# Gate and up projections by a seven-product block scheme, with the weight sums on VectorE

## The reference, cut to what matters

```python
for l in range(DEPTH):                      # DEPTH = 1, D_MODEL = 1024, D_FF = 2816
    h = rms_norm(x, norm_mix[l])
    ...                                     
    x = x + merged @ w_out[l]
    h = rms_norm(x, norm_ffn[l])
    x = x + (jax.nn.silu(h @ w_gate[l]) * (h @ w_up[l])) @ w_down[l]
return rms_norm(x, norm_final)
```

## Time and profile before

| | |
|---|---|
| median of three runs | 1140.46 us |
| the profiled execution, its own time | 1147.27 us |
| span of its slowest core (core 3, the one shown) | 1145.7 us |
| spans of the other cores | 1136.1 to 1139.3 us |
| granted TensorE clock, mean of core 3 | 0.996 of 2.4 GHz |
| PE busy | 1121.7 us (98%) |
| DVE busy | 475.8 us (42%) |
| ACT busy | 305.6 us (27%) |
| POOL busy | 79.1 us (7%) |

### The profile page before, as it was taken

The page is one execution under the profiler, slowest core; times in us unless marked ns, Lnnn a source line. Parts: engine busy times, 40 slices in busy tenths (PEclk is TensorE's granted clock), DMA queues, the critical chain, the costliest instruction groups (busy, mean ns, idle before and its releaser), DMA issues.

```text
span 1145.7 us, 14700 instructions; the slowest of 8 cores (1136.1 to 1145.7 us)
## 1 busy us (share of the span) xinstructions
PE 1121.7 (98%) x5574; PEld 542.3 (47%) x5574; DVE 475.8 (42%) x482; ACT 305.6 (27%) x490; POOL 79.1 (7%) x153
## 2 busy tenths in 40 slices
PE   7999999998999999999999999999999999999998
PEld 3666545453454444444444444444444444444444
DVE  5453554553656556553545622111334211111223
ACT  5434444224212323421212110112432111111111
POOL 1110100100100010001000101111000000000000
PEclk9999999998999999999999999999999999999999
DMA  9999881688498989335415543999967354200133
GB/s 244 172 203 162 132 206 47 114 147 107 83 191 195 258 150 173 61 106 111 76 39 107 95 142 103 219 175 173 173 154 193 102 126 77 37 1 1 37 112 109
DMA packets 78916, 146.34 MB, mean 128 GB/s; under 512 B 46571, under 2 KB 46571, under 8 KB 78592
## 3 DMA queue, kind: packets, MB, share of 16 engines
q0 software_dynamic: 21456, 77.64, 40.1%
q1 hardware_dynamic: 57392, 67.78, 21.7%
HBM read 185.27 MB, written 23.07 MB: 182 GB/s over the span
## 4 chain that ended last, share of the span: by engine, by line
PE 90%; DMA 4%; DVE 3%; ACT 1%; issue 1%; SPq 0%; DVEq 0%; ACTq 0%
PE ps L228 90%; DMA arena<-hb 3%; DMA arena<-x 1%; ACT tmp L419 1%; DVE tmp L390 0%; DVE hb L331 0%; DVE tmp L470 0%; DVE smx L416 0%; PE ps L343 0%; DVE tmp L383 0%; DVE arena L397 0%; ACT tmp L387 0%; ACT hA L352 0%; SPq L177 0%; DVE tmp L483 0%
## 5 line engine op out<-in xcount | busy, mean ns | idle before, releaser
L228 PE MATMUL ps<-hA,ring 128*128 128x512 bf16 (+3 forms) x2496 | 509.0, 364 | 9.1 <-DMA ring<-w_in 5.1
L228 PEld LDWEIGHTS ps<-hA,ring 128*128 128x128 bf16 x2496 | 243.7, 98 | 266.8 <-issue 14.2
L228 PE MATMUL ps<-arena,ring 128*128 128x512 bf16 (+1 forms) x1600 | 330.7, 366 | 0.8 <-ACT tmp L419 0.8
L228 PEld LDWEIGHTS ps<-arena,ring 128*128 128x128 bf16 x1600 | 156.5, 98 | 170.5 <-issue 1.1
L228 PE MATMUL ps<-arena 128*128 128x512 bf16 (+1 forms) x854 | 181.3, 374 | 0.0
L629 DVE TENSOR_TENSOR arena<-ps,tmp 128x1024 bf16<-128x1024 f32 x44 | 53.9, 1225 | 227.9 <-PE ps L228 223.9
L228 PEld LDWEIGHTS ps<-arena 128*128 128x128 bf16 x854 | 83.5, 98 | 96.3
L625 ACT ACTIVATE tmp<-ps 128x1024 f32<-128x1024 f32 x44 | 45.1, 1025 | 253.5 <-PE ps L228 253.5
L470 DVE TENSOR_TENSOR tmp<-tmp 128x1024 f32<-128x1024 f32 (+6 forms) x40 | 49.2, 1230 | 41.1 <-ACT tmp L460 38.6
L228 PE MATMUL ps<-ring,arena 128*128 128x512 bf16 x256 | 57.9, 379 | 0.2 <-issue 0.2
L218 POOL DMA_DIRECT2D ring<-w_in x48 | 25.6, 541 | 442.3 <-PE ps L228 333.4
(11 more groups left out here) (98 smaller groups left out, 585.3 us busy)
## 6 DMA issues: line engine op xcount, KB each, us to landing
ring<-w_in POOLq DMA_DIRECT2D x48, 512.0 KB, 12.9
ring<-w_gate_up POOLq DMA_DIRECT2D x44, 512.0 KB, 12.2
arena<-x SPq DMA_DIRECT2D x32, 512.0 KB, 7.2
tmp<-x_scr SPq DMA_DIRECT2D x24, 512.0 KB, 4.8
x_scr<-arena SPq DMA_DIRECT2D x16, 512.0 KB, 3.3
out<-tmp SPq DMA_DIRECT2D x15, 512.0 KB, 3.1
arena<-w_down POOLq DMA_DIRECT2D x11, 512.0 KB, 24.6
ring<-w_kv POOLq DMA_DIRECT2D x8, 512.0 KB, 18.6
```

Of the source, the lines that this page charges most:

```text
L228: ins = e.matmul(o, l, r, start=s0, stop=s1)
```

## The change

`gu_g` and `gu_u` give way to `gate_up`. Weights and input of a chunk are taken as 2 by 2 blocks (gate and up by channel blocks 0 to 3 and 4 to 7; channel halves by token halves), and the four output blocks come from seven products of four matmuls, 28 instead of 32, over three banks, two of which take two products each. Sums of input blocks are made once for a half (`x_sums`): three go into ring slots that are held from then on, two are written over blocks of `HA`. Sums of weight blocks (`w_sums`) are made for each chunk on DVE while the chunk before it runs, in two parts: `one` and `two`; three blocks go into the space of `kT` or `vT`, two are written over their slot. Each chunk's products are combined by ACT and DVE. The last multiplication of a chunk is put behind the next chunk's second ACT copy (`late`), its silu behind the next chunk's first (`late_act`). The output tiles of half 1 move to chunks 2 to 5, the norms of half 1 all go beside the down tiles, and the last norm of `ffn(0)` goes behind the first sums of `ffn(1)`.

```diff
@@ -165,7 +165,7 @@
     PS = nc.alloc_psum_tensor("ps", [P, 4096], F32)
     plan = Plan()
     st = {"slot": 0, "pb": 0, "stat": 0, "hb": 0, "sm": 0}
-    held = set()
+    held, slots_held = set(), set()
 
     def act(fn, reads, writes):
         plan.op("act", fn, reads=reads, writes=writes)
@@ -205,6 +205,8 @@
             return (self.kind, self.i)
 
     def slot_new():
+        while st["slot"] % RING in slots_held:
+            st["slot"] += 1
         s = Ref("S", st["slot"] % RING)
         st["slot"] += 1
         return s
@@ -620,14 +622,124 @@
...
-    def gu_g(c, s):
-        u = Unit(lambda kc: rg(s, kc * P, (kc + 1) * P), s, (H0.rhs, H0.keys)).run()
-        act(lambda e: e.activation(out=T[c % 2][:, 0:TM], in_=u.ps(), func=AF.Silu), u.keys(), [("T", c % 2)])
-
-    def gu_u(c, s):
-        u = Unit(lambda kc: rg(s, 1024 + kc * P, 1024 + (kc + 1) * P), s, (H0.rhs, H0.keys)).run()
-        dve(lambda e: e.tensor_tensor(out=actT[:, c, :], in0=u.ps(), in1=T[c % 2][:, 0:TM], op=ALU.mult),
-            u.keys() + [("T", c % 2)], kA(c))
+
+    xq = {}
+
...
+
+    def x_slots():
+        for n in ("11+22", "21+22", "11+12"):
+            xq[n] = slot_new()
+            slots_held.add(xq[n].key()[1])
+
+    def x_sums(p):
+        x11, x12, x21, x22 = x_view(0, 0, p), x_view(0, 1, p), x_view(1, 0, p), x_view(1, 1, p)
+        lo, hi = [("HA", p + 1)], [("HA", p + 5)]
+
+        def dst(n):
+            return ring[:, xq[n].key()[1], :].rearrange("p (k t) -> p k t", k=4)[:, :, p * P:(p + 1) * P]
+
...
+        tt(dst("11+22"), x11, x22, ALU.add, lo + hi, [xq["11+22"].key()])
+        tt(dst("11+12"), x11, x12, ALU.add, lo, [xq["11+12"].key()])
+        n2 = dst("21+22")
+        dve(lambda e: e.scalar_tensor_tensor(out=n2, in0=x21, scalar=-1.0, in1=x22, op0=ALU.mult, op1=ALU.subtract),
+            hi, [xq["21+22"].key()])
+        tt(x12, x12, x22, ALU.subtract, lo + hi, lo)
+        tt(x21, x21, x11, ALU.subtract, lo + hi, hi)
+
+    wx = [kT[:, :, :].rearrange("p k t -> p (k t)"), vT[:, :, :].rearrange("p k t -> p (k t)")]
+    wxk = [[("kT",)], [("vT",)]]
+
+    def w_sums(c, s):
+        e_, ek = wx[c % 2], wxk[c % 2]
+        sk = [s.key()]
+        w = rg(s, 0, SW)
+        pairs = w.rearrange("p (a b) -> p a b", a=2)
+        w11, w22 = rg(s, 0, 512), rg(s, 1536, 2048)
+        quads = w.rearrange("p (a b) -> p a b", a=4)
+        mid = rg(s, 512, 1536).rearrange("p (a b) -> p a b", a=2)
+        def one():
+            dve(lambda e: e.tensor_tensor(out=e_[:, 0:1024], in0=pairs[:, 0, :], in1=pairs[:, 1, :], op=ALU.add), sk, ek)
+
+        def two():
+            dve(lambda e: e.tensor_tensor(out=e_[:, 1024:1536], in0=w11, in1=w22, op=ALU.add), sk, [("wA", c % 2)])
+            dve(lambda e: e.tensor_tensor(out=mid, in0=quads[:, 0:4:2, :], in1=quads[:, 1:4:2, :], op=ALU.subtract), sk, sk)
+        return one, two
+
+    late, late_act = [], []
+
+    def gate_up(c, s, Q, sums):
+        e_, ek, wa = wx[c % 2], wxk[c % 2], [("wA", c % 2)]
+        q4, q5, q3, q1, q2 = Q
+        T4, T5, T3, T1, T2 = [T[q] for q in Q]
+        k5, k3, k1 = [("T", q5)], [("T", q3)], [("T", q1)]
+        ks, kt, k2l, k2r = [("T", q4)], [("q4r", q4)], [("T", q2)], [("q2r", q2)]
+        lo, hi = [("HA", t) for t in range(1, 5)], [("HA", t) for t in range(5, 9)]
+        bA = banks(3)
+        bC, bD = bA + 1, bA + 2
+
...
+        def prod(b, w, x, first):
+            mms = [(bank(b), w[0](k), x[0](k), first and k == 0, k == 3) for k in range(4)]
+
+            def fn(e):
+                ins = None
+                for (o, l, r, s0, s1) in mms:
+                    ins = e.matmul(o, l, r, start=s0, stop=s1, skip_group_check=True)
+                return ins
+            plan.op("pe", fn, reads=w[1] + x[1], writes=kB(b, 1))
+
+        def cp(o, b, wr, fn=AF.Copy, sc=1.0, rd=()):
+            act(lambda e: e.activation(out=o, in_=bank(b), func=fn, scale=sc), kB(b, 1) + list(rd), wr)
+
...
+        L, R = slice(0, 512), slice(512, 1024)
+        prod(bC, ws_(512), xh(1, 1), True)
+        cp(T4[:, L], bC, ks)
+        while late_act:
+            late_act.pop(0)()
+        prod(bD, ws_(1536), xs_("11+12"), True)
+        tt(T4[:, R], bank(bD), T4[:, L], ALU.add, kB(bD, 1) + ks, kt)
+        if sums:
+            sums[0]()
+        prod(bA, we(1024, wa), xs_("11+22"), True)
+        tt(T5[:, L], bank(bA), T4[:, R], ALU.subtract, kB(bA, 1) + kt, k5)
+        prod(bD, ws_(1024), xh(0, 0), False)
+        cp(T1[:, L], bD, k1)
+        while late:
+            late.pop(0)()
+        if sums:
+            sums[1]()
+        prod(bC, ws_(0), xs_("21+22"), False)
+        prod(bA, we(512, ek), xh(0, 1), True)
+        two = T5[:, L].unsqueeze(1).broadcast_to((P, 2, 512))
+        o2 = T3[:, 0:1024].rearrange("p (a b) -> p a b", a=2)
+        ac = bank(bA, 2).rearrange("p (a b) -> p a b", a=2)
+        tt(o2, ac, two, ALU.add, kB(bA, 2) + k5, k3)
+
+        def silu():
+            cp(T2[:, R], bC, k2r + k2l, AF.Silu, -1.0, k3)
+            act(lambda e: e.activation(out=T2[:, L], in_=T3[:, L], func=AF.Silu), k3, k2l)
+        late_act.append(silu)
+        prod(bD, we(0, ek), xh(1, 0), False)
+        tt(T1[:, R], bank(bD), T3[:, R], ALU.add, k3 + kB(bD, 1), k1)
+        late.append(lambda: tt(actT[:, c, :], T1[:, 0:TM], T2[:, 0:TM], ALU.mult, k1 + k2l + k2r, kA(c)))
...
@@ -871,8 +983,20 @@
...
+    gu0 = []
+
     def s_hook(j, pos):
         s_tail()
+        if j in (4, 5) and pos == 2:
+            if j == 4:
+                x_slots()
+            x_sums(2 * (j - 4))
+            x_sums(2 * (j - 4) + 1)
+        if j == 6 and pos == 0:
+            gu0.extend(slot_load(w_gu_d[c]) for c in range(2))
+        if j == 7 and pos == 1:
+            for w in w_sums(0, gu0[0]):
+                w()
 
     def merge(hf, H, first):
...
-    sO = [slot_load(w_out_d[q]) for q in range(4)]
+    sO = []
     for i in range(3):
         o_load(1, i)
     TB = [2, 3, 4, 5, 6]
+    roles = [[0, 1, 2, 3, 4, 5, 6], [0, 1, 2, 3, 4, 5, 6]]
...
+    CO = (0, 4, 1, 5, 2, 6, 3, 7)
+
     def ffn(hf):
-        gu = [slot_load(w_gu_d[c]) for c in range(4)]
-        cp, cq = [], []
+        gu = list(gu0)
+        while len(gu) < 4:
+            gu.append(slot_load(w_gu_d[len(gu)]))
+        gu0.clear()
+        if hf == 0:
+            sO.extend(slot_load(w_out_d[q]) for q in range(4))
         for c in range(NF):
-            if c + 4 < NF:
-                gu.append(slot_load(w_gu_d[c + 4]))
             if hf == 0 and c in WD:
                 q = 2 * WD.index(c)
                 dst = atoms(NF + q, 2)
                 plan.op("pool", lambda e, dst=dst, q=q: e.dma_start(out=dst, in_=w_down_d[:, q * D:(q + 2) * D]),
                         writes=kA(NF + q, 2), dma=True)
-            gu_g(c, gu[c])
-            o1(hf, 2 * c)
-            gu_u(c, gu[c])
-            o1(hf, 2 * c + 1)
-            if hf == 0 and NF - 8 <= c < NF - 5:
-                cq.append(x1_load(1, c - NF + 8))
-            if hf == 0 and NF - 6 <= c < NF - 3:
-                q = cq.pop(0)
-                n_ = Norm(T[q][:, 0:D], [("T", q)])
-                cp.append((n_.finish(), c - NF + 6))
+            r = roles[hf]
+            gate_up(c, gu[c], r[:3] + r[3 + 2 * (c % 2):5 + 2 * (c % 2)],
+                    w_sums(c + 1, gu[c + 1]) if c + 1 < NF else None)
+            if c >= 2 and hf == 0 and 2 * c - 4 < NT:
+                while late_act:
+                    late_act.pop(0)()
+                o1(hf, 2 * c - 4)
+                o1(hf, 2 * c - 3)
+            if c + 4 < NF:
+                gu.append(slot_load(w_gu_d[c + 4]))
+        for w in late_act + late:
+            w()
+        late.clear()
+        late_act.clear()
+        cq, cp, cx = [], [], []
+        ydq = [x1_load(hf, 0)]
         if hf == 0:
-            cq.append(x1_load(1, 3))
-            nxt = [3, 4]
-        ydq = [x1_load(hf, 0)]
+            cq = [(x1_load(1, t), t) for t in CO[0:2]]
         for i in range(NT):
             b = banks(2)
+            if hf == 0:
+                for p in cx:
+                    x_sums(p)
+                cx = []
+                for b_, t in cp:
+                    c_trans(b_, t)
+                    if t >= 4:
+                        cx.append(t - 4)
+                cp = []
+                if 1 <= i <= 4:
+                    for q2, t in cq:
+                        cp.append((Norm(T[q2][:, 0:D], [("T", q2)]).finish(), t))
+                    cq = [(x1_load(1, t), t) for t in CO[2 * i:2 * i + 2]]
+                if i == 1:
+                    gu0.extend(slot_load(w_gu_d[c]) for c in range(4))
+                if i == NT - 1:
+                    for w in w_sums(0, gu0[0]):
+                        w()
 
             def grp(kcs, nbs=(0, 1)):
                 return [(bank(b + nb), actT[:, kc, i * P:(i + 1) * P], wdT[:, kc, nb * 512:(nb + 1) * 512],
@@ -994,26 +1145,21 @@
                 continue
```

(56 more changed lines are left out.)

## The result

The changed kernel takes **1121.49 us** (median of four, 1120.12 to 1121.98) against 1140.53 for the kernel before beside it: the ratio is **0.9831, 95% interval 0.9818 to 0.9843**, 19 us less. The forecast was 1121. The profiled execution took 1121.98 us, its span is 1120.4 (core 0).

The account below looks back on a forecast made before the run. PE's matmul count was taken to bound these stages. Terms -22.9 (shorter chunks), +0.6 (start of `ffn(0)`) and +2.6 (moved norm) gave -19.7 us, from the median 1140.46 to 1121; range of 8 in 10: 1112 to 1136.

Parts of the forecast that it names:

- Part 1: Gate and up chunks: 4 of 32 matmuls go in each of 44 chunks, 38.0 us off; PE's chunk 6.04 us.
- Part 2: DVE's load per gate and up chunk: fast bf16 sums, 6.34 us, 6.03 with joins, as long as PE's 6.04.
- Part 3: Latency chain inside a gate and up chunk: period 6.385 us instead of 6.906, 22.9 us gained over 44 chunks.
- The wait at P4: PE's wait before each chunk's fourth product, until DVE's addition has read its bank: 0.31 us in every chunk.
- the 13.6 and the 1.5: Of the 38.0 us, 13.6 lost to waits before the fourth product, 1.5 to waits for the second weight-sum part.
- Part 4 and 7: Output tiles of half 1 in chunks 2 to 5, and input sums in merge and down tiles: both cost 0.
- Part 5: Start of `ffn(0)`: the merge's last DVE operation delays chunk 0's first DVE addition, 0.6 us lost.
- Part 6: Moved norm in `ffn(1)` chunk 0: it delays the weight sums and chunk 1's first product, 2.6 us lost once.
- Part 8: Weight loads with nine slots left: they land in time, room 2.4 us at the least; cost 0, at most 3.
- rival C: Weight loads come late in the gate and up burst: +14 us, 1135; chance 0.06.
- Rivals B and D: Longer DVE joins and releases: 1130 to 1135, chance 0.13; falling clock: 1123, or far over 1140 with chance 0.03.
- Rival D: Clock falls behind PE waits: +2.4 us after the 2.6 wait, 1123; from 0.3 us waits far over 1140, chance 0.03.

Follow-up runs that it names:

- the late P7: Changed kernel with a chunk's seventh product issued behind the next chunk's second and DVE's order changed: stages -14.3 us, ratio to the kernel before 0.9732.
- the two moves: Changed kernel with the seventh product late, DVE reordered and the last norm's ACT part early: stages -14.7 us, ratio to before 0.9711, again 0.9785.

## Why the prediction was right

**Part 1.** Right: 5398 weight loads against 5574, and 6.04 us per chunk is reached as soon as the waits go.

**Part 2.** Right on the point on which the sign hung. `one`, the short sum and the long one last 0.68, 0.416 and 0.692 us; forecast 0.692, 0.425, 0.692. The first half of the perf-mode rule that the prediction cites from the Trainium skill (VectorE: DVE Perf Modes, the perf-mode tier table), which no row of before could show, holds here: 692 ns for 1024 bf16 elements. The joins too: 958.47 - 957.87 = 0.60 for an operation of 0.69.

**Part 3.** Right in kind, 1% off in size. The wait at P4 is 0.25 to 0.31 against 0.31, the period 6.32 against 6.385. What the hand schedule shows with 0.03 at the next P1, and what I read as a small rest, is in truth the second way, of the same length: removing the "13.6 us of the P4 wait" alone gives nothing. That reading of the 13.6 and the 1.5 as two separate losses is the step that was wrong, though the period and the sum do not rest on it.

**Part 4 and 7.** Output tiles and input sums cost nothing; the cover of the sums is larger than what they need.

**Part 5.** Forecast 0.6, measured 0.7: T4R of the first chunk starts 2.78 after the first product (651.50 to 654.28; forecast 2.69), and the chunk takes 7.06 instead of 6.32. The list names 0.86 for P4's wait there and 0.15 for an ordinary one.

**Part 6.** Forecast 2.6; the list names 2.37, and by the spacing of the products it is 2.5. Its cause, the reciprocal behind ACT, is shown. What I missed is the next chunk: ACT loads its table before its first silu, 1.28 us, the product of the chunk before gets late, and with it the sums; PE waits 0.51 in `ffn(0)` and, on the four cores whose clock stayed up, 0.50 in `ffn(1)`. The rows, in `ffn(1)`:

```profile
906.24 1.28 ACT L708 ACT_TABLE_LOAD   x1
...
908.96 1.22 DVE L711 TENSOR_TENSOR arena<-tmp 128x1024 bf16<-128x1024 f32 x1 [0.56 <-ACT tmp L738]
...
911.46 0.81 PE L703 MATMUL ps<-hA,ring 128*128 128x512 bf16 x3 [0.50 <-DVE ring L670]
```

**Part 8 and rival C.** No wait of DVE or PE in these loops names a DMA. POOL did run into its limit of eight, but the weights were there.

**Rivals B and D.** The joins and releases were as the rows said. The clock did not fall in the steady chunks. Behind the one wait of 2.4 us it did, on four of eight cores, and it cost them 0.7 to 1.0 us; on core 0, the one that the page shows, the products step by 0.86 again from 904.45 on. Rival D had allowed for this with up to 2.4. In all the runs that have that wait (2.4 us and more) the clock fell there on four to eight cores, and in the five that do without it on none. The Trainium skill's case of frequent short waits that lower the clock (TensorE: Matmul & The Clock Gate, A second HAM failure mode) did not come up with some forty waits of 0.3 us.

**The number.** That 1121 met 1121.49 so closely is in part luck. The stages gained 1.1 us more than forecast. The shorter period gives some 2.5 us more over both halves; the two waits behind ACT's table loads, which I had not seen, take back 0.6 to 0.7 each, and part 5 and the clock some tenths. The longer last stage and the slowest core then brought the total down to 19.

Two of my expectations in the experiments were off: the late P7 gave 14 us and not 9 to 11, since I had not counted that the new order on DVE also frees the sums from the norm (2.5 us in the run that moves only them, the clock included); and for the same reason the two moves did not add.

## What to carry to other kernels

Trading matmuls for vector work pays by what the waits between engines leave, not by the matmuls taken away: write one period of the loop out by hand, with the measured lag of each release, and look for every closed way through it, not only for the first wait. Where two ways are of equal length, shortening one shows nothing, and an operation that has no hurry (the last product, the last multiplication) belongs behind the one that releases the next round.

## What the runs showed of the hardware that was not expected

`scalar_tensor_tensor` on bf16 data from SBUF to SBUF takes 683 ns for 512 elements and 1225 for 1024, one element per step, where `tensor_tensor` takes 416 and 692. In this kernel the choice between the two forms of one and the same subtraction is worth 49 us.

A DVE operation that waits for PE has one of two lags. In 329 of the changed kernel's 352 chunks (22 in each half, on eight cores) T4R starts 0.27 us (196 times) or 0.34 us (133 times) after P2's last slot, and PE's wait at P4 is nearly always 0.25 with the first and 0.31 with the second. How long DVE had been idle does not decide it: the shorter lag stands behind pauses of 0.07 to 0.50 us, the longer behind 0.14 and more. What decides it stays open.

In one execution of one program, the clock fell behind a single wait of 2.4 us on four cores and not on the other four, and the wait cost those four up to 1.0 us more than its own length. Why it fell on some cores and not on others stays open.
